# Feed-forward output: the high and low left tiles in one 512-column matmul for five of seven products, with VectorE's work in another order

## The reference

```python
def swiglu(h, w_in, w_out):
    gate, up = jnp.split(h @ w_in, 2, axis=-1)
    return (jax.nn.silu(gate) * up) @ w_out          # w_out: 2816 x 1024

for layer in range(2):
    x = x + 0.5 * swiglu(rmsnorm(x, g1), w_ffn1_in, w_ffn1_out)
    x = x + mixer(rmsnorm(x, g))                     # retention, then sparse attention
    x = x + 0.5 * swiglu(rmsnorm(x, g2), w_ffn2_in, w_ffn2_out)
return rmsnorm(x, final_norm)
```

## Time and profile before

| | us |
|---|---|
| median of 3 runs | 1927.34 |
| lowest, highest | 1926.14, 1927.45 |
| the profiled execution | 1926.12 |
| its span, first to last instruction | 1924.1 |
| TensorE busy | 1906.3 (99%) |
| VectorE busy | 1591.0 (83%) |
| ScalarE busy | 992.2 (52%) |

### The profile page before, as it was taken

One profiled execution on the slowest core, in us unless ns is written; L12 is line 12 of the kernel. 1 busy time (PEld: TensorE's weight loads), 2 busy tenths in 40 slices (PEclk: granted clock), 3 DMA queues, 4 the chain that ended last, 5 costly groups with the idle time before them and its releaser, 6 DMA issues.

```text
span 1924.1 us, 27006 instructions
## 1 busy us (share of the span) xinstructions
PE 1906.3 (99%) x10772; PEld 1664.5 (87%) x10772; DVE 1591.0 (83%) x1905; ACT 992.2 (52%) x1298; POOL 188.8 (10%) x164
## 2 busy tenths in 40 slices
PE   9999999999999999999999999999999999999998
PEld 7888899888888888888899888889997898888998
DVE  8988896986767859889896988989768768988985
ACT  6554555452434435545655555564568445555642
POOL 0000000000000032000000000000036440000000
PEclk9999999999999999999999999999999999999999
DMA  6776855231313333677845576784422018667852
GB/s 232 197 214 214 234 188 195 105 137 44 137 44 137 107 112 91 216 197 201 270 145 180 178 234 181 206 268 140 177 85 88 1 45 261 199 190 201 264 183 86
DMA packets 100524, 316.63 MB, mean 165 GB/s; under 512 B 5936, under 2 KB 14128, under 8 KB 97328
## 3 DMA queue, kind: packets, MB, share of 16 engines
q1 hardware_dynamic: 82704, 222.35, 32.5%
q0 software_dynamic: 17408, 92.28, 19.4%
q10 hardware_dynamic: 288, 0.29, 0.1%
HBM read 312.80 MB, written 94.37 MB: 212 GB/s over the span
## 4 chain that ended last, share of the span: by engine, by line
PE 91%; DVE 4%; ACT 1%; issue 1%; DMA 1%; POOL 1%; SPq 0%; DVEq 0%; POOLq 0%; ACTq 0%
PE bank L2855 13%; PE bank L2857 13%; PE bank L2856 13%; PE bank L3028 7%; PE bank L3030 7%; PE bank L3029 7%; PE bank L2847 4%; PE bank L2849 4%; PE bank L2848 4%; PE bank L3084 3%; PE bank L3086 3%; PE bank L3085 3%; PE bank L2961 2%; PE bank L3095 1%; PE bank L3347 1%
## 5 line engine op out<-in xcount | busy, mean ns | idle before, releaser
L1212 ACT ACTIVATE part_hi<-quad_w 128x1024 fp32r<-128x1024 f32 x280 | 293.2, 1064 | 278.5 <-PE bank L2857 195.8
L1825 DVE TENSOR_TENSOR part_lo<-quad_w,part_hi 128x1024 fp32r<-128x1024 f32 x280 | 329.8, 1217 | 23.6 <-ACT part_hi L1212 23.4
L2855 PE MATMUL bank<-part_hi,s_hi 128*128 128x512 f32 x640 | 252.5, 394 | 0.7 <-DVE part_lo L1825 0.6
L2857 PE MATMUL bank<-part_hi,s_lo 128*128 128x512 f32 x640 | 249.6, 390 | 0.0
L2856 PE MATMUL bank<-part_lo,s_hi 128*128 128x512 f32 x640 | 249.3, 390 | 0.0
L2855 PE MATMUL bank<-part_hi,xn_hi 128*128 128x512 f32 x608 | 237.6, 391 | 0.8 <-DVE part_lo L1877 0.8
L2857 PE MATMUL bank<-part_hi,xn_lo 128*128 128x512 f32 x608 | 236.7, 389 | 0.0
L2856 PE MATMUL bank<-part_lo,xn_hi 128*128 128x512 f32 x608 | 236.7, 389 | 0.0
L1992 DVE TENSOR_TENSOR quad_w<-quad_w,quad_w 128x1024 f32<-128x1024 f32 x160 | 188.5, 1216 | 1.1
L1239 ACT ACTIVATE part_hi<-quad_w 128x1024 fp32r<-128x1024 f32 x84 | 87.0, 1058 | 148.5 <-PE bank L2849 105.9
L2857 PEld LDWEIGHTS bank<-part_hi,s_lo 128*128 128x128 f32 x640 | 120.1, 188 | 25.2
(11 more groups left out here) (411 smaller groups left out, 5023.3 us busy)
## 6 DMA issues: line engine op xcount, KB each, us to landing
quad_w<-w_ffn_in SPq DMA_DIRECT2D x80, 1024.0 KB, 7.5
t_sums<-w_ffn_out POOLq DMA_DIRECT2D x48, 1408.0 KB, 10.2
t_sums<-t_sums POOLq DMA_DIRECT2D x16, 1408.0 KB, 6.5
quad_w<-w_ret_in SPq DMA_DIRECT2D x14, 1024.0 KB, 7.5
first_raw<-w_ffn_out SPq DMA_DIRECT2D x16, 704.0 KB, 8.2
out_raw_C<-t_sums SPq DMA_DIRECT2D x12, 704.0 KB, 4.3
rest_raw<-w_ffn_in SPq DMA_DIRECT2D x32, 256.0 KB, 5.8
quad_w<-w_ret_in SPq DMA_DIRECT2D x16, 512.0 KB, 5.0
```

Source lines behind the costliest of these rows:

```text
L1212: nc.scalar.activation(in_four(part_hi[part_slot(h)]), source, copy).then_inc(part_hi_made, 1)
L1825: nc.vector.tensor_tensor(in_four(part_lo[part_slot(h)]), source, in_four(part_hi[part_slot(h)]).bitcast(FP32), ALU.subtract)\
L2855: mm(to, hi, in_four(part_hi[slot])[:, :, part], start=start, stop=False, skip_group_check=joins)
L2857: return mm(to, lo, in_four(part_hi[slot])[:, :, part], start=False, stop=stop, skip_group_check=joins)
```

## The change

For the five products S1T1, S2T2, S3T3, x22T4 and S4w22, `w_hi` meets both left tiles in one matmul of 512 columns (`left_parts`: the high tile's 256 columns and the low tile's, taken from one arena at two offsets); `w_lo` still meets the high tile alone. A step's results then fill a bank of their own: one half for `w_hi` with the tile that lies first and for `w_lo`, the other for `w_hi` with the second tile. x11w11 and x12w21 keep their three matmuls, and so does step 3 of chain Z in the last feed-forward (`one_width`). To make room, V and Z share the four upper banks, so S1T1 waits for P2, and the last transposes go to these banks too. `add_out` adds both halves by two instructions, the second of which waits for the first (`link`).

VectorE's list is changed: P1a later, P2 earlier, P5 to after the low piece of step 19, P6a to before that of step 16, P6b to before that of step 18. The first weights of retention and of sparse attention are split, on ScalarE and VectorE, before step 26's piece instead of after step 27's; ahead of a feed-forward its first weights are split one place earlier; the additions for retention's S1 come after the end of the stage. Loads stand in the same order as before on SyncE and GpSimd.

```diff
-X_ADDS = ["x11 P1 a", "x11 P1 b", "x11 P2 a", "x11 P2 b", "x22 P5 a", "x22 P5 b",
-          "x12 P6 a", "x12 P6 b", "x22 P7 a", "x22 P7 b"]
+X_ADDS = ["x11 P1 a", "x11 P1 b", "x11 P2 a", "x11 P2 b", "x12 P6 a", "x12 P6 b",
+          "x22 P5 a", "x22 P5 b", "x22 P7 a", "x22 P7 b"]
...
-    bank = [ctx.enter_context(nc.psum_tensor(f"bank{n}", [P, SEQ], FP32)) for n in range(8)]
+    banks = ctx.enter_context(nc.psum_tensor("banks", [P, 8 * SEQ], FP32))
+    bank = [banks[:, SEQ * n:SEQ * (n + 1)] for n in range(8)]
...
+    def left_parts(p, k):
+
+
+        both = sorted([left_hi_at[p % 2] + 4 * HALF_SEQ * k, left_low_at(p, k)])
+        return bass.AP(left_arena, (both[0] - arena_at) // 4,
+                       [[arena_width, P], [(both[1] - both[0]) // 4, 2], [1, HALF_SEQ]])
...
+    def one_width(s, p, dt):
+
+
+        return OUT_PRODUCTS[p] in ("x11w11", "x12w21") \
+            or chain_of(p) == "Z" and s == len(SUBLAYERS) - 1 and dt == OUT_TILES - 1
...
-        if chain == "Z" and s == len(SUBLAYERS) - 1 and dt == OUT_TILES - 1:
-            return 6, 0
-        first = {"Y": 0, "V": 2, "Z": 4}[chain]
-        if s + 1 < len(SUBLAYERS) and SUBLAYERS[s + 1] == "ret":
-            first = {"Y": 0, "V": 4, "Z": 2}[chain]
-        return first + dt // 2, dt % 2
+        return dt if chain == "Y" else upper_banks(s)[dt]
...
                     square(0)
                     square(1)
+                    if following == "ret":
+                        split_ret("q", 0, 0)
+                        split_ret("q", 0, 1)
+                    elif following == "dsa":
+                        for n in range(3):
+                            raw, hi, _ = dsa_first(s + 1, n)
+                            act.wait_ge(*unit_loads(u0 + OUT_STEPS + (1 if n else 0)))
+                            nc.scalar.activation(hi, raw, copy).then_inc(first_hi_parts, 1)
                     out_high(i + 2)
...
                     square(3)
                     if following == "ret":
-                        split_ret("q", 0, 0)
-                        split_ret("q", 0, 1)
                         for k in range(HALF_CHUNKS):
                             scaled_copy(s + 1, k)
-                    elif following == "dsa":
-                        split_unit(u0 + OUT_STEPS)
+                    elif following == "ffn":
+                        rest(s + 1, 0)
                     residual(s, 4)
                     residual(s, 5)
...
-                    made = bank[n][:, :].rearrange("p (d t) -> p d t", d=2)[:, first:first + b - a]
+                    made = banks[:, SEQ * n:SEQ * (n + b - a)].rearrange("p (d i t) -> p d i t", d=b - a, i=2)
                     dve.wait_ge(unit_done, u0 + OUT_TILES * p + b)
-                    done = nc.vector.scalar_tensor_tensor(to, made, factor, to, ALU.mult, ALU.add)
+                    done = nc.vector.scalar_tensor_tensor(to, made[:, :, 0], factor, to, ALU.mult, ALU.add)
+                    if not one_width(s, p, a):
+                        link(done)
+                        done = nc.vector.scalar_tensor_tensor(to, made[:, :, 1], factor, to, ALU.mult, ALU.add)
...
-                add_out("x11", 0, two[0], "P1", 0.5)
                 out_low(4)
                 out_low(5)
                 left_low(1, 0)
                 left_low(1, 1)
+                add_out("x11", 0, two[0], "P1", 0.5)
                 sum_left("S1")
                 out_low(6)
                 add_out("x11", 0, two[1], "P1", 0.5)
                 out_low(7)
                 left_low(2, 0)
+                dve.wait_ge(x_added, x_added_count(s, "x11 P1 a"))
+                add_out("x11", 1, two[0], "P2", 0.5)
                 out_low(8)
                 left_low(2, 1)
                 out_low(9)
-                sum_left("S2")
-                dve.wait_ge(x_added, x_added_count(s, "x11 P1 a"))
-                add_out("x11", 1, two[0], "P2", 0.5)
-                out_low(10)
-                out_low(11)
                 dve.wait_ge(x_added, x_added_count(s, "x11 P1 b"))
                 add_out("x11", 1, two[1], "P2", 0.5)
+                out_low(10)
+                sum_left("S2")
+                out_low(11)
                 left_low(3, 0)
                 out_low(12)
                 left_low(3, 1)
                 out_low(13)
                 sum_left("S3")
-                add_out("x22", 2, pieces(s, "Z")[0], "P5", 0.5)
                 out_low(14)
                 out_low(15)
-                for piece in pieces(s, "Z")[1:]:
-                    add_out("x22", 2, piece, "P5", 0.5)
                 left_low(4, 0)
+                add_out("x12", 3, two[0], "P6", -0.5)
                 out_low(16)
                 left_low(4, 1)
                 out_low(17)
+                add_out("x12", 3, two[1], "P6", -0.5)
+                out_low(18)
                 sum_left("S4")
-                add_out("x12", 3, two[0], "P6", -0.5)
-                out_low(18)
                 out_low(19)
-                add_out("x12", 3, two[1], "P6", -0.5)
+                for piece in pieces(s, "Z"):
+                    add_out("x22", 2, piece, "P5", 0.5)
...
                     stream_lo(s + 1, 1)
                     add_square(1)
+                    if following == "ret":
+                        split_ret("q", 0, 0)
+                        split_ret("q", 0, 1)
+                    elif following == "dsa":
+                        first_low(0)
+                        first_low(1)
+                        first_low(2)
...
+            if s > 0 and SUBLAYERS[s - 1] == "ffn":
+                pe.wait_ge(x_updated, CHUNKS * (s - 1) + OUT_TILES + 2)
...
+                    elif name == "S1T1":
+                        pe.wait_ge(x_added, x_added_count(s, f"x11 P2 {ab}"))
...
-                    to = cols(bank[n], first, HALF_SEQ)
-                    opens = name in ("x11w11", "x12w21", "S1T1") and dt == piece[0]
-                    closes = dt == piece[1] - 1
-                    joins = name in ("S2T2", "S3T3", "x22T4", "S4w22")
+                    both = bank[out_bank(s, chain, dt)]
+                    to = cols(both, 0, HALF_SEQ)
+                    opens = name in ("x11w11", "x12w21", "S1T1")
+                    joins = not opens
                     _, hi, lo = out_bufs(i)
                     batches = [a for a, _ in LEFT_BATCHES[p]]
                     for k in range(HALF_TILES):
                         if dt == 0 and k in batches:
                             pe.wait_ge(left_lo_made, left_count(f, p, batches.index(k)))
-                        left_hi_k, left_lo_k = cols(left_hi[p % 2], k, HALF_SEQ), left_low_tile(p, k)
-                        first_in, last_in = opens and k == 0, closes and k == HALF_TILES - 1
+                        left_hi_k = cols(left_hi[p % 2], k, HALF_SEQ)
+                        first_in, last_in = opens and k == 0, k == HALF_TILES - 1
                         w_hi_k, w_lo_k = hi[:, k * P:(k + 1) * P], lo[:, k * P:(k + 1) * P]
-                        mm(to, w_hi_k, left_hi_k, start=first_in, stop=False, skip_group_check=joins)
-                        mm(to, w_hi_k, left_lo_k, start=False, stop=False, skip_group_check=joins)
+                        if one_width(s, p, dt):
+                            mm(to, w_hi_k, left_hi_k, start=first_in, stop=False, skip_group_check=joins)
+                            mm(to, w_hi_k, left_low_tile(p, k), start=False, stop=False, skip_group_check=joins)
+                        else:
+                            mm(both.rearrange("p (n t) -> p n t", n=2), w_hi_k, left_parts(p, k),
+                               start=first_in, stop=False, skip_group_check=joins)
                         done = mm(to, w_lo_k, left_hi_k, start=False, stop=last_in, skip_group_check=joins)
```

110 lines of the change are left out of this document (57 added, 53 removed).

## The result

The changed kernel takes 1951.81 us (median; 1949.09 to 1952.68) beside 1926.78 us for the kernel before on the same chip: ratio 1.0127, 95% interval 1.011 to 1.0145. It is slower, by about 25 us where 15 were forecast, and lies 1.8 us above the upper end of the range. The profiled execution took 1949.09 us, span 1947.3, so 23.2 us more than the span before. It is the fastest of the four, 2.7 us under the median, and what follows explains this execution, not the median.

The account below looks back on a forecast made before the run. TensorE, busy 99% of the span, was taken as the bound. Hand-over terms +7.5, +7.5, +0.4 and -0.3 made +15.1 us on 1926.1, giving 1941.2, told as 1942; eight-in-ten range 1931 to 1950.

Parts of the forecast that it names:

- 858 x 0.013 = 11.2 us: Output stages: 858 merged matmul pairs each give back 0.013 us of TensorE time, making steps 3.82 us instead of 3.96.
- The bound from four runs of 128 columns: Wide matmul over two far runs: earlier matmuls reading four runs took 0.227 us, so no extra cost was taken.
- rival (c): Wide matmul over two far runs costs 0.240 us, steps stay 3.96: 1950 us, slower; chance 0.10 together with (d).
- The stall before step 20: Each output stage: TensorE waits 2.4 us for a late VectorE addition to x, 9.7 us in all.
- M16: The moment SyncE sees step 15 of an output stage ended; forecast 1.14 us earlier than before.
- Retention: Change from feed-forward to retention, once: stalls of 4.1 us before step 26 and 1.8 before step 27; +7.5 us together.
- M24: The moment SyncE sees step 23 of an output stage ended; forecast to stand where it stood in every stage.
- The attention: Change to the sparse attention, once: same order as at retention, its weight load landing at 7.25 instead of 6.5; +7.5 us.
- Next feed-forward and last stage: Pairs lengthen VectorE's tail ahead of the next feed-forward, +0.4 us; the last stage's steps from 24 gain, -0.3 us.
- (a): Rival: the waits don't bite and only the merge shows: 1916 us, faster; chance 0.06.
- (b): Rival: step 20 stalls, but query and attention weights land before they hold anything: 1927 us, no change; chance 0.09.
- (d): Rival: VectorE's reads over two banks cost 0.1 us more each: 1948 us; chance 0.10 together with rival (c).

Follow-up runs that it names:

- experiment 5: The changed kernel with the wide matmul reading two neighbouring high tiles, one run of 512 columns, the low tile's share left out: 1950.78 us, ratio 1.0132.
- experiment 7: The kernel with first weights' pieces and P5 additions both moved back, merge kept, with the two matmuls of every other left tile turned about: 1921.58 us.
- Experiment 2: The changed kernel with the P5 additions back behind the low piece of step 15, ahead of the P6 additions: 1938.53 us, ratio 1.0061.
- experiment 4: The changed kernel's order without the merge: every wide matmul as two narrow ones, each addition one operation: 1939.78 us, ratio 1.0071.
- experiment 6: The changed kernel with 33 and 44 extra matmuls ahead of step 26's wait in the first and third output stages: 1950.73 us, ratio 1.0124.
- experiments 3 and 10: 3: the changed kernel with first weights' pieces and P5 additions both moved back, 1925.02 us; 10: the same without the merge, 1925.81 us.
- experiment 1: The changed kernel with the next stage's first weights' pieces back behind the squares on ScalarE and VectorE: 1938.46 us, ratio 1.0065.

## Why the forecast was right in kind and too small

**The merge: mis-sized.** The step that failed is "858 x 0.013 = 11.2 us", 3.82 us a step. Steps took 3.886: 0.0067 a pair, 5.8 us in all. The bound from four runs of 128 columns did hold, a wide matmul over two far runs costs nothing more (experiment 5); rival (c) was wrong in its cause. What the sum left out is that wide among wide and narrow among narrow, the two paces that the rows had, say nothing on wide and narrow in turn. There the same stream runs in one of two rhythms, 3.886 or 3.813 a step (the last two timelines under experiment 7; 3.813 is near the 3.82 forecast), and it ran nearly always in the slower. So step 24 came 1.0 to 1.15 us later after the stage's start in three stages where I had it unmoved: with the second stage's share 4.4 us of the 8.1 that the profiled execution lies above the sum. The median, which left the range, lies another 2.7 us higher, and no trace shows why; without the 4.4 us it would be 1947.4, inside.

**The stall before step 20: right.** Forecast 2.4 us in each stage and step 20 at M16 + 17.6. SyncE saw step 15 ended at 294.81, and step 20 began at 312.47: 17.66. Stalls 2.3, 2.3, 2.3 and 2.1 us, released by the second operation of P7a's pair; a pair's distance 0.72 for the 0.71 of the earlier trace rows. (The prediction speaks of five pairs in this stretch; its own list has four, and the sum uses four.) Experiment 2 took P5 out of that row, and P7a was done at 309.62 with step 20 at 310.02: the place in the queue is shown as the cause. That pair and position are both needed is what experiment 4 shows. Not foreseen: the clock's lower level behind the wait in the second stage, 1.5 us.

**Retention: right, 1.1 us short.** Forecast stalls of 4.1 and 1.8 us; the trace has 4.0 to 4.2 before step 26, and experiment 6 lays the second bare, 1.65. In the changed kernel itself the slow clock filled that second stall's place. Step 27 began 18.0 us after M24 and not 17.1, but that is not what was missing: experiment 6 took 0.7 of it away and the next stage came 0.1 sooner. What counts is VectorE's chain. Its low piece for step 27 was done at M24 + 17.3 as forecast (17.1); from there to TensorE's sum over squares it took 11.5 us where I had 10.9, so that the sum came at 28.8 and not 28.0. In that chain the second operation of a pair starts 0.79 to 0.80 after the first, not 0.71. The last 0.3 lie behind the sum.

**The attention: right, 2.4 us short.** I took the weight's load at 6.4 us from the earlier trace rows, and the first of two loads as nothing. They took 5.9 and 7.9, each 1.5 longer than before, and the high piece of step 26 was started at M24 + 10.6 where 9.2 would follow from my terms (7.25 + 2.0): 1.4 of the 2.4. Another 0.5 is the state before: I took TensorE's sum over squares at M24 + 21.7 from the retention side, and ahead of the attention it had come at 21.2 (1398.39). The slow clock of step 26 counts for 0.3 (experiment 6).

**Next feed-forward and last stage:** forecast +0.4 and -0.3, measured -0.5 and -0.2.

**The rivals.** (a), waits that don't bite, and (b), only step 20, fell with the two new waits. (c) had the size of the result, 1950, from a wrong cause. (d), dearer reads of two banks, fell too: an operation of a pair takes 0.68 to 0.69 us, as in the earlier trace rows.

**What I would not have found in the profile before:** that the merge is worth almost nothing even where nothing waits for it (0.8 us, experiments 3 and 10), because the two hand-overs hang on VectorE's queue. The forecast had booked the pairs there at 0.7 or 0.8 each but set them against a saving of 11 and not of 6.

Not settled: what chooses between the two rhythms. Behind the wait before step 20 the slower one ended in two stages of four in experiment 1, three in experiment 5, one in experiment 6 and none in the changed kernel, with and without a fall of the clock.

## What to carry to other kernels

Before moving an operation ahead in an in-order queue, ask for each instruction behind it what it waits for: here raw data that were ready stood 8 and 10 us behind a load that landed later. A merge that saves on the bounding engine but splits its consumer's work in two pays with the consumer's latency wherever the bounding engine waits for it at a hand-over; count those places first. Take the pace of a mixed stream from a mixed stream, and try the order of its members: it was worth about 3 us here.

## What the runs showed of the hardware

Wide and narrow matmuls in strict turn, each with new weights, have two stable rhythms at the same granted clock of 1.00: starts 0.347 us a pair, 0.230 behind each wide one, or 0.353 with distances of 0.232, 0.236 and 0.241 in rotation behind the wide one. Turned about in pairs they take 0.348.

After waits of 3.7 us or more (two each in the changed kernel and experiments 2, 4 and 5) TensorE's granted clock was at 0.56 to 0.73 over the step that followed, eight times of eight, and the next step began 5.4 to 6.6 us later instead of 3.9. In experiment 6, whose extra matmuls filled all but 0 and 0.4 us of the same two waits, it stayed at 1.00. After waits of 1.9 to 2.1 us it fell in one stage of four in the changed kernel and in two of four in each of experiments 1, 5 and 6, to 0.69 over the step. The Trainium skill (TensorE: Matmul & The Clock Gate, section What's actually happening) says that the clock's share follows how busy the engine has been of late; these rows agree with it. What such a fall costs is read from what is late next: 1.5 us behind step 20, and next to nothing behind step 26.
